# Scores of the diagonal and of next neighbours as elementwise products summed by a matrix of ones

## The reference

```
q = silu(xn @ w_q);  forget = lb + (1 - lb) * sigmoid(xn @ w_f)
log_f = log(forget);  k = 1 - forget;  v = xn @ w_i
b = cumsum(log_f)                       # within a chunk
scores[t, s] = sum_d q[t, d] * k[s, d] * exp(b[t, d] - b[s, d])    for s <= t
o = scores @ v + (q * exp(b)) @ state
state = exp(b_last) * state + (k * exp(b_last - b)).T @ v
o = rmsnorm(o, g_norm) * silu(xn @ w_g);   out = o @ w_o
```

## Time and profile before

| | |
|---|---|
| median of 3 runs | 2187.16 us (2186.94 to 2187.41) |
| profiled execution | 2187.14 us, span 2185.3 us |
| TensorE busy | 2168.1 us, 99% |
| VectorE busy | 1458.3 us, 67% |
| ScalarE busy | 998.5 us, 46% |
| GpSimd busy | 939.0 us, 43% |
| granted TensorE clock, mean | 1.00 |

### The profile page before, as it was taken

How to read it: one execution, slowest core, us unless ns; L and a number is a source line. 1 busy time by engine, 2 the same in 40 slices (tenths; PEclk the granted TensorE clock), 3 DMA queues, 4 the chain that set the end, 5 groups by cost and what they waited for, 6 DMA issues and landing times.

```text
span 2185.3 us, 30303 instructions
## 1 busy us (share of the span) xinstructions
PE 2168.1 (99%) x11542; PEld 1831.3 (84%) x11542; DVE 1458.3 (67%) x1980; ACT 998.5 (46%) x1364; POOL 939.0 (43%) x263
## 2 busy tenths in 40 slices
PE   8999999999999999999999999999999999999998
PEld 6888887787898897888887898898788888898897
DVE  6999998667556468878777565467666514566462
ACT  5353554524343344665655342344566524342343
POOL 3444445544553554333133553554411244553552
PEclk9999999999999999999999999999999999999999
DMA  6233332422223333222213323233322233233331
GB/s 200 96 106 106 106 110 88 140 96 96 97 97 99 110 101 107 58 78 58 58 58 97 97 97 97 97 107 89 102 53 58 68 88 97 97 97 97 98 113 71
DMA packets 230851, 206.67 MB, mean 95 GB/s; under 512 B 13904, under 2 KB 220368, under 8 KB 230480
## 3 DMA queue, kind: packets, MB, share of 16 engines
q1 hardware_dynamic: 227328, 199.36, 29.4%
q10 hardware_dynamic: 3408, 5.70, 0.7%
HBM read 194.02 MB, written 4.19 MB: 91 GB/s over the span
## 4 chain that ended last, share of the span: by engine, by line
PE 92%; issue 4%; POOL 2%; ACT 1%; DVE 1%; DMA 0%; POOLq 0%; SPq 0%; ACTq 0%; DVEq 0%
PE ps L2027 15%; PE ps L2029 15%; PE ps L2028 15%; PE ps L2260 6%; PE ps L2258 6%; PE ps L2259 6%; PE ps L2060 5%; PE ps L2061 5%; PE ps L2062 5%; PE ps L2387 2%; POOL w_lo L647 2%; PE ps L2594 2%; PE ps L2555 2%; PE ps L2583 1%; PE ps L2690 1%
## 5 line engine op out<-in xcount | busy, mean ns | idle before, releaser
L647 POOL TENSOR_TENSOR w_lo<-raw,w_hi 128x2048 fp32r<-128x2048 f32 x145 | 692.3, 4774 | 949.2 <-ACT w_hi L697 938.8
L697 ACT ACTIVATE w_hi<-raw 128x2048 fp32r<-128x2048 f32 x144 | 275.8, 1915 | 533.4 <-PE ps L2029 357.4
L2027 PE MATMUL ps<-FH,w_hi 128*128 128x512 f32 x528 | 208.6, 395 | 0.0
L2028 PE MATMUL ps<-FL,w_hi 128*128 128x512 f32 x528 | 208.6, 395 | 0.0
L2029 PE MATMUL ps<-FH,w_lo 128*128 128x512 f32 x528 | 208.6, 395 | 0.0
L2027 PE MATMUL ps<-XH,w_hi 128*128 128x512 f32 x512 | 203.5, 397 | 0.0
L2029 PE MATMUL ps<-XH,w_lo 128*128 128x512 f32 x512 | 202.3, 395 | 0.0
L2028 PE MATMUL ps<-XL,w_hi 128*128 128x512 f32 x512 | 202.2, 395 | 0.0
L660 POOL TENSOR_TENSOR w_lo<-raw,w_hi 128x1024 fp32r<-128x1024 f32 x39 | 107.9, 2766 | 198.2 <-ACT w_hi L891 198.2
L1604 DVE TENSOR_TENSOR ps<-ps,rst 128x1024 f32<-128x1024 f32 (+1 forms) x52 | 55.5, 1066 | 173.4 <-PE ps L2029 124.1
L1340 DVE SCALAR_TENSOR_TENSOR ps<-UP,vec,ps 128x512 f32<-128x512 f32 x224 | 148.6, 743 | 0.0
(11 more groups left out here) (435 smaller groups left out, 5888.1 us busy)
## 6 DMA issues: line engine op xcount, KB each, us to landing
raw<-in_w SPq DMA_DIRECT2D x64, 512.0 KB, 4.3
raw<-in_mlp_w_up SPq DMA_DIRECT2D x64, 512.0 KB, 4.4
raw<-in_mlp_w_down SPq DMA_DIRECT2D x64, 512.0 KB, 4.3
raw<-in_w_in SPq DMA_DIRECT2D x56, 512.0 KB, 4.6
raw<-in_mla_w_o SPq DMA_DIRECT2D x16, 512.0 KB, 5.1
raw<-in_w_b_out SPq DMA_DIRECT2D x16, 384.0 KB, 4.0
raw<-in_w_a_out SPq DMA_DIRECT2D x8, 512.0 KB, 4.5
raw<-in_w_o SPq DMA_DIRECT2D x8, 512.0 KB, 4.0
```

The costliest lines, as they stand in the source:

```text
L647: pool.tensor_tensor(w_lo[:, s], raw[:, s], w_hi[:, s].bitcast(F32), ALU.subtract)\
L697: act.activation(w_hi[:, s], raw[:, s], ACT.Copy).then_inc(hi_done, 1)
L2027: pe.matmul(dst, his[k], xh[k], start=start and k == 0, stop=False)
L2028: pe.matmul(dst, his[k], xl[k], start=False, stop=False)
```

## The change

Two of the eight float32 score products of each head are replaced. For the diagonal, VectorE makes `HD = HQ * HK`, ScalarE its rounded part `HDH`, VectorE the rest `HDL`; TensorE sums them over the features with two fp32r matmuls of 512 columns against a matrix of ones, which gives every partition the column's sum, of which the mask keeps the one wanted. For the level m = 1 only the second token of each pair gets an argument and an exponential; VectorE multiplies it by the key before and, in a second step that waits for the first, by the query (`HN`), ScalarE makes `HNH`, VectorE `HNL`, and TensorE sums with two matmuls of 256 columns. `HNH` is made behind `HV` and the weight split ahead of it, `HNL` behind the states. The new tiles have memory of their own and reuse finished semaphores.

```diff
             def diagonal(h):
 
                 pe.wait_ge(s_("h_t1"), h + 1)
-                pe.wait_ge(s_("hq_done"), h + 1)
-                for b in range(TB):
-                    t = slice(b * P, (b + 1) * P)
-                    mm = pe.matmul(ps[:, 6, t], HK[:, t], HQ[:, t], start=True, stop=True)
-                mm.then_inc(s_("h_g"), 1)
+                pe.wait_ge(*ff("h_one", 1))
+                pe.wait_ge(*ff("h_dl", h + 1))
+                pe.matmul(ps[:, 6], ONES[:], HDH[:], start=True, stop=False)
+                pe.matmul(ps[:, 6], ONES[:], HDL[:], start=False, stop=True).then_inc(s_("h_g"), 1)
...
                 pe.wait_ge(s_("h_qk"), 14 * h + 2 * l + 2)
+                if m == 1:
+                    pe.wait_ge(*ff("h_nl", h + 1))
+                    pe.matmul(ps[:, 4 + l % 2, 0:HALF], ONES[:], HNH[:], start=True, stop=False)
+                    pe.matmul(ps[:, 4 + l % 2, 0:HALF], ONES[:], HNL[:], start=False, stop=True)\
+                        .then_inc(s_("h_g"), 1)
+                    return
...
                 for l in range(len(LEVELS)):
                     act.wait_ge(s_("h_arg"), 14 * h + 2 * l + 2)
-                    act.activation(HE[:, l], HE[:, l], ACT.Exp).then_inc(s_("h_e"), 1)
+                    e = HE[:, l] if l < len(LEVELS) - 1 else HE[:, l].rearrange("p (g u) -> p g u", u=2)[:, :, 1]
+                    act.activation(e, e, ACT.Exp).then_inc(s_("h_e"), 1)
+                act.wait_ge(*ff("h_d", h + 1))
+                act.activation(HDH[:], HD[:], ACT.Copy).then_inc(ff_sem("h_dh"), 1)
+
+            def next_act(h):
+
+                act.wait_ge(s_("h_qk"), 14 * h + 14)
+                act.activation(HNH[:], HN[:], ACT.Copy).then_inc(ff_sem("h_nh"), 1)
...
+                if not first:
+                    next_act(h)
                 act.wait_ge(s_("h_kt"), h + 1)
...
+                    if m == 1:
+                        dve.tensor_tensor(ev[:, :, 1], bv[:, :, 1], bv[:, :, 0], ALU.subtract).then_inc(s_("h_arg"), 2)
+                        continue
...
+                    if m == 1:
+                        next_ = HN[:].rearrange("p (g t) -> p g t", t=1)
+                        dve.tensor_tensor(next_, ev[:, :, 1], kv[:, :, 0], ALU.mult).then_inc(ff_sem("h_n"), 1)
+                        dve.wait_ge(*ff("h_n", h + 1))
+                        dve.tensor_tensor(next_, next_, qv[:, :, 1], ALU.mult).then_inc(s_("h_qk"), 2)
+                        continue
...
+            def same_dve(h):
+
+                dve.wait_ge(s_("hq_done"), h + 1)
+                dve.wait_ge(s_("hk_done"), h + 1)
+                dve.tensor_tensor(HD[:], HQ[:], HK[:], ALU.mult).then_inc(ff_sem("h_d"), 1)
+
+            def same_low_dve(h):
+
+                dve.wait_ge(*ff("h_dh", h + 1))
+                dve.tensor_tensor(HDL[:], HD[:], HDH[:].bitcast(F32), ALU.subtract).then_inc(ff_sem("h_dl"), 1)
+
+            def next_low_dve(h):
+
+                dve.wait_ge(*ff("h_nh", h + 1))
+                dve.tensor_tensor(HNL[:], HN[:], HNH[:].bitcast(F32), ALU.subtract).then_inc(ff_sem("h_nl"), 1)
...
                 states_dve(h, n)
+                next_low_dve(h)
                 levels_dve(h, (5,))
...
                 levels_dve(h, (7,))
                 if more:
+                    same_dve(h + 1)
                     decays_dve(h + 1, range(3, len(LEVELS)))
                     keys_to_end_dve(h + 1, 1 - n)
                     rest_dve(h + 1, 1 - n)
                     decayed_dve(h + 1, 1 - n)
+                    same_low_dve(h + 1)
                 dve.wait_ge(s_("h_inv"), h + 1)
...
             decays_dve(0, range(len(LEVELS)))
+            same_dve(0)
             keys_to_end_dve(0, 0)
             decayed_dve(0, 0, range(2), last=False)
+            same_low_dve(0)
             rest_dve(0, 0)
```

More of the change, by code:

```diff
@@ L196, in build_program @@
             ("FR", [P, T], F32),
+            ("HD", [P, T], F32), ("HDH", [P, T], F32R), ("HN", [P, HALF], F32), ("HNH", [P, HALF], F32R),
+            ("ONES", [P, P], F32R),
         ]
@@ L202, in build_program @@
             at_h += size + (-size) % 32
-        HR, HZ, HQ, HK, HF, HGATE, HVF, HV, HE, HP, HQD, HKD, HEB, reset, HKT, HS, masks, FR = made
+        HR, HZ, HQ, HK, HF, HGATE, HVF, HV, HE, HP, HQD, HKD, HEB, reset, HKT, HS, masks, FR, HD, HDH, HN, HNH, ONES = made
+        HDL, _ = place("HDL", [P, T], F32R, at_h - (4 * T + 4 * T + 4 * HALF + 4 * HALF + 4 * P))
+        HNL, _ = place("HNL", [P, HALF], F32R, at_h - (4 * HALF + 4 * HALF + 4 * P))
         AH, _ = place("AH", [P, HEADS_M, T], F32R, a_xh)
@@ L275, in build_program @@
             "part_kept": ("lru_done", 15), "u_y": ("mu_add", 7), "u_f": ("xc_done", 8), "u_fh": ("uh_done", 8),
-            "u_fl": ("yb_evac", 8), "root_2": ("ch_done", 2), "d_scaled": ("v_part", 36),
+            "u_fl": ("yb_evac", 8), "root_2": ("ch_done", 2), "h_d": ("lam_abs", 2), "h_dh": ("ln_inv", 2), "h_dl": ("pads", 2),
+            "h_n": ("mu_mm", 1), "h_nh": ("var_mm", 1), "h_nl": ("r_row", 1), "h_one": ("lam_e", 1), "d_scaled": ("v_part", 36),
         }
@@ L976, in _ @@
             mlp_act("mlp0", after_mlp0)
+            act.activation(ONES[:], ones[:], ACT.Copy).then_inc(ff_sem("h_one"), 1)
             act.wait_ge(s_("f_gain"), 2)
@@ L1058, in head_act @@
                     gates_act(h + 1, split=(lambda: split_hi(2 * h + c + 4, 0)) if first else None)
+                if first:
+                    next_act(h)
                 out_gate_act(h, n)
```

## The result

| | before | changed |
|---|---|---|
| median | 2187.22 us (2186.94 to 2187.41, 4 runs) | 2200.65 us (2200.17 to 2201.45, 4 runs) |
| ratio | | 1.0062, interval 1.0051 to 1.0074 |
| profiled execution | 2187.14 us, span 2185.3 | 2201.45 us, span 2199.7 |
| TensorE busy | 2168.1 us, 99% | 2166.1 us, 98% |
| period of an alike head | 33.38 us | 34.65 us |

The change makes the kernel 13.4 us slower. 9.4 had been forecast, and 2200.65 lies just outside the range (2189 to 2200). The direction, the mechanism and, within 0.15 us, the length of an alike head came out as forecast; one term, head 7, was far too small.

What follows compares the result with a forecast made beforehand. TensorE, 99% busy, bounds it, with a loop through VectorE, GpSimd and ScalarE nearly as long (32.8 against 33.38 us). Head 1 +2.9, five intervals +5.5, head 7 +1.7, last level -0.7: +9.4, so 2196.5 us, range 2189 to 2200.

Steps and rivals of the forecast that it cites:

- level 1 of head 1: Head 1's level 1 on TensorE, at 935.34 before, comes 2.9 us later, with head 0's delay and the port wait.
- five intervals: From head 1's level 1 to head 6's: 172.5 us (5 x 34.5) instead of 167.0, so +5.5 us.
- the hole: Gap in VectorE's row before the second HN product; GpSimd's split takes the shared port there, tmp times HGATE ending +1.68 us.
- a sign against it: TensorE's step is wrong if the two 512-column matmuls take over 0.47 us or the 256-column pair over 0.24.
- the old one plus 1.7 us: Loop through VectorE, GpSimd, ScalarE and TensorE's level 1 in each alike head: 32.8 + 1.7 = 34.5 us against 33.38.
- The old slack of 0.1: VectorE's copy ahead of the outputs ends at 983.74, the outputs would start at 984.0: some 0.1 us of slack now.
- Head 7's level 1, at 1133.16, already stands behind HV and takes the 1.7 once more: Head 7's level 1 on TensorE: bound by HV, another 1.7 us late, bringing the sum from +8.4 to +10.1.
- some 1.0 of it falls before the diagonal: Alike heads: of 2.2 us TensorE idle, some 1.0 before the diagonal, waiting for the norm product, the rest before level 1.
- The first: Rival: VectorE keeps the port until HDL ends, the split comes after; loop 33.8, +4.5, 2191.6 us; chance 0.25.
- The second, on the other side: Rival: VectorE's tail is off the path, TensorE keeps its saving; -8.7, 2178.5 us, half kept 2183 to 2187; chance 0.15.
- The third: Rival: both holes and a later copy for the outputs, 0.2 to 0.4 us more a head; 2198 to 2200; chance 0.10.
- the second loop: Alike heads: VectorE's row, GpSimd's split, tmp times HGATE, ScalarE's HV, TensorE's level 1; 32.8 us long, slack 0.55.

Runs made afterwards that it cites:

- the first experiment: Changed kernel with HQD placed between the two HN products in heads 1 to 7: 2192.23 us, ratio 1.0023.
- the diagonal's part alone: Kernel before with only the diagonal replaced (HD, HDH, HDL), last level as before: 2195.26 us, ratio 1.0041.
- the extra matmuls: Changed kernel with 16 unused 512-column matmuls in head 7 between the transposes and the diagonal: 2198.82 us, ratio 1.0055.
- three edits: Changed kernel with HQD between the HN products, HV and HNH ahead of the second weight split, X's scaling behind the next head's copy of index 4: 2185.11 us.
- the last level's part alone: Kernel before with only the last level replaced (HN, HNH, HNL), diagonal as float32 products: 2184.16 us, ratio 0.9986.
- The last two kernels: Three edits plus head 0's float32 diagonal, 2182.94 us; the same with HV copied ahead of OH in head 7, 2183.07 us.
- the two slices: Changed kernel with 12 of head 7's output projection products (two slices) moved ahead of its diagonal: 2197.77 us, ratio 1.0052.
- head 0's diagonal as before: Kernel with the three edits, but head 0's diagonal as the four float32 products of the kernel before: 2182.94 us, ratio 0.9981.
- both edits: Changed kernel with HQD between the HN products and with HV and HNH ahead of the second weight split: 2188.24 us, ratio 1.0005.
- the last one: Kernel with three edits and head 0's float32 diagonal, plus HV copied ahead of OH in head 7: 2183.07 us, ratio 0.9981.

## Why the prediction was right and wrong

| step | forecast | measured |
|---|---|---|
| diagonal, two matmuls of 512 columns | 0.47 us | 0.56 us behind a wait, 0.55 without one |
| saved by the diagonal's part on TensorE | 0.42 us | 0.42 us |
| last level, two of 256 columns | 0.24 us | 0.12 + 0.12 |
| GpSimd's request behind the mean | 4.31 us | 4.30 us |
| second HN product | about 4.8 us, in heads 1 to 7 | 4.70 to 4.78 us |
| `tmp` times `HGATE` | 0.7 us | 0.69 us |
| end of that behind the mean | 11.78 us | 11.78 us |
| TensorE idle per alike head | 2.2 us | 1.25 + 0.93 us |
| level 1 of head 1 | +2.9 us | 938.75 - 935.34 - 0.5 = +2.9 us |
| five intervals | 172.5 us | 173.3 us |
| head 7's level 1, against head 6's | +1.7 us | +5.2 us |
| last level, to the end | -0.7 us | -0.6 us |
| sum | +9.4 us | +13.8 us (profiled run, 0.5 taken off), +13.4 (medians) |

**Right:** who gets the port, when, and what is late behind it. The chain read from the earlier trace rows held to a few hundredths, and the first experiment shows that the hole is its cause. The diagonal's saving is right in part by luck: its two matmuls take 0.55 us even where nothing waits (1002.23 to 1002.78 in the diagonal's part alone), more than the 0.47 that the prediction had named as a sign against it, but the transpositions ahead of them hold 0.08 less than ahead of the float32 diagonal (0.25 to the next start instead of 0.33).

**The small miss, +0.8 over five intervals.** The loop was taken as the old one plus 1.7 us. Measured, level 1 to the next mean matmul takes 1027.77 - 1008.08 = 19.69; the rows before give 1022.38 - 1002.20 = 20.18, less 0.66 for the last level: 19.52. Of the 0.17 between them, 0.1 is level 1 itself (a record of 1.10 us behind the wait, 1.00 where nothing waited); the rest I can only argue: the outputs wait a little for VectorE's last copy in some heads. The old slack of 0.1 there had been seen, and was given to a rival instead of to the sum.

**The step that failed: "Head 7's level 1, at 1133.16, already stands behind HV and takes the 1.7 once more".** It carried the alike heads' bound over to a head whose order differs. Head 7 has fewer products ahead of its diagonal. The norm product's end moved from 5.09 us behind the mean matmul (994.09 - 989.00) to 11.06 (1004.18 - 993.12), by 5.97. In the alike heads TensorE reached the diagonal 10.02 behind the mean (999.02), with 4.93 to spare, so 1.0 is left to wait (1.25 by the starts, with the 0.13 from the norm product's end to the diagonal and the 0.08 just named). In head 7 it was there 7.21 behind the mean (1129.75 against 1122.54), with 2.12 to spare, and of the same 5.97 some 3.8 are left (3.7 in the row above). The bound of level 1 is then no longer HV (its copy ends at 1144.62, and level 1 could follow at 1144.75) but norm product, diagonal, level 0 and six products: 1142.80 + 2.76 = 1145.56, 0.8 later than HV plus 0.13. The other 2.5 us, to 1148.09, is the half clock, which stands nowhere in the prediction. So of the 3.5 us missed, 2.5 is the clock and 1.0 the changed bound (0.8 of it by these rows); the extra matmuls gave back 1.8 to 2.6 by the clock alone. I had worked out this wait for the alike heads ("some 1.0 of it falls before the diagonal") and did not ask the same of head 7.

**The rivals.** The first (hole missed, loop 33.8, 2191.6 us) is what the kernel with HQD between the products does: 33.76 and 2192.23 us, though that run has the half clock in it, which the rival had not. The second, on the other side, was wrong for the change as made: its condition, VectorE's tail off the path, isn't met; with the tail taken off the path by three edits the alike heads keep 0.84 us. The third (more waits) came nearest in time, for another reason than it named.

## What to carry to other kernels

A dependent pair on an engine that shares a port with another costs more than its 0.1 us of waiting, if the other's request can fall into the gap: put an independent operation between the two. Work taken from the busiest engine and given to one at 67% is no gain when that engine's queue is the second loop; find that loop's slack (here 0.55 us of 33.38) and compare it with what is added ahead of the operation that closes it (here 1.0 to 1.2). And work the sum out anew for the first and the last turn of a loop, whose order and slack are others.

## What the runs showed of the hardware

**A gap of 0.1 us is enough.** In all seven heads from 1 on the split started 0.12 to 0.15 us before the second HN product, which took 4.3 us longer than the 0.43 of head 0. In head 0 no request fell there, with the same gap ahead of the product. In the last level's part alone the request came 0.46 us behind the product's start, with HQD under way, and had to wait: its 5.05 us are 0.44 more than 4.61, to within 0.13 of HQD's end. A product held off this way ended 0.29 us behind the split; `tmp` times `HGATE` of 512 columns did so by 0.54. The remainder goes with the width, so the product seems to run in full once the port is free; that is an inference from two rows.

**The clock after a short wait isn't the same each time.** After 3.7 us of waiting it fell to 0.50, in one profile for longer than in the other (above). After 1.6 us it fell in some profiles and not in others. The kernel with HQD between the products, head 7 (a wait for the split, then the products behind it):

```profile
1134.00:1136.30 2.30, 0.70 (x7) 0.56 (x6) 2.30 (x1) 0.00 (x0) 2.30 (x1) 1.00 0.00 0
1136.40:1138.60 2.20, 2.20 (x5) 1.79 (x6) 1.38 (x3) 1.72 (x4) 0.00 (x0) 0.50 0.33 110
```

and the kernel with X's scaling later, the same place:

```profile
1127.60:1129.40 1.80, 0.23 (x3) 0.10 (x1) 1.80 (x1) 0.00 (x0) 1.80 (x1) 1.00 0.00 0
1129.50:1132.00 2.50, 2.46 (x13) 1.85 (x14) 1.68 (x3) 1.97 (x5) 0.00 (x0) 1.00 0.47 128
```

The products' pitch is 0.43 us in the first and 0.23 in the second, for waits of the same length. The last two kernels repeat it: TensorE's operations are the same up to the wait, 1.68 and 1.66 us of it in head 7, and behind it 1.00 in one profile and 0.50 in the other (1128.5 to 1131.0).

The mean granted clock of each execution, which is on record, goes with this scatter. With X's scaling later, the execution at 0.997 took 2186.76 us, the four at 0.998 took 2185.22 to 2185.67 and the six at 0.999 took 2184.26 to 2185.11. With HQD between the products, the three at 0.998 took 2192.62 to 2193.37 and the eight at 0.999 took 2190.57 to 2192.57. With the two slices, the two at 0.998 took 2199.37 and 2199.81 and the other three at most 2197.77. With head 0's diagonal as before, the only one at 0.998 took 2185.31 and the ten at 0.999 at most 2183.22. In the kernel with both edits and in the last one the ranges overlap. So one part of the scatter between executions of one kernel is the clock; in which wait it fell no record of an execution without a profile says, and what decides the case stays open.
